# Dilated attention's probabilities: turned by VectorE in 32x32 squares and placed through DRAM, in place of TensorE transposes

## The reference, cut to what matters

```python
# per pattern: tokens of one residue modulo dil, in blocks of BLK = 128
s = einsum('bnqhd,bnkhd->bnhqk', q, k_prev_and_own) * 64 ** -0.5     # 128 queries x up to 256 keys
s = where(valid, s, -inf)
m = max(s); e = exp(s - m); l = sum(e)
o = einsum('bnhqk,bnkhd->bnqhd', e / l, v_prev_and_own)
lse = m + log(l)         # the three patterns' outputs are then weighted by softmax(lse)
```

## Time and profile before

| what | before |
|---|---|
| median of 3 runs | 3045.55 us (3045.34 to 3045.76) |
| profiled execution, its span | 3043.6 us |
| TensorE, VectorE, ScalarE, GpSimd busy | 99%, 69%, 35%, 64% |
| DMA | 301.71 MB in 367379 packets, mean 99 GB/s |
| TensorE's mean granted clock | 0.999 of full |

### The profile page before, as it was taken

How to read it: one execution, slowest core, us unless ns; L and a number is a source line. 1 busy time by engine, 2 the same in 40 slices (tenths; PEclk the granted TensorE clock), 3 DMA queues, 4 the chain that set the end, 5 groups by cost and what they waited for, 6 DMA issues and landing times.

```text
span 3043.6 us, 40003 instructions
## 1 busy us (share of the span) xinstructions
PE 3025.0 (99%) x14420; PEld 2448.4 (80%) x14420; DVE 2085.4 (69%) x2848; ACT 1057.5 (35%) x1911; POOL 1951.7 (64%) x1630
## 2 busy tenths in 40 slices
PE   8999999999999999999999999999999999999999
PEld 7777888888888888778888888888888777788887
DVE  6656585556888865565665558888769988797223
ACT  4223253333444421233343334444331345302112
POOL 5632458888999557433558878998545544486574
PEclk9999999999999999999999999999999999999999
DMA  5112234446444221112144456544111100111112
GB/s 167 51 42 50 74 108 160 152 153 246 154 152 166 82 84 51 48 43 87 50 140 153 152 187 213 154 148 151 47 44 49 35 28 22 32 49 49 46 63 83
DMA packets 367379, 301.71 MB, mean 99 GB/s; under 512 B 66640, under 2 KB 302160, under 8 KB 365648
## 3 DMA queue, kind: packets, MB, share of 16 engines
q1 hardware_dynamic: 318432, 222.33, 24.0%
q10 hardware_dynamic: 48752, 76.83, 7.3%
HBM read 223.29 MB, written 72.68 MB: 97 GB/s over the span
## 4 chain that ended last, share of the span: by engine, by line
PE 97%; DVE 2%; ACT 0%; issue 0%; DMA 0%; SPq 0%; DVEq 0%; ACTq 0%
PE ring L1581 14%; PE ring L1583 14%; PE ring L1582 14%; PE ring L1862 4%; PE ring L1863 4%; PE ring L1864 4%; PE ring L1895 4%; PE ring L1897 4%; PE ring L1896 4%; PE aux L1581 3%; PE aux L1583 3%; PE aux L1582 3%; PE aux L1895 2%; PE aux L1897 2%; PE aux L1896 2%; PE aux L1862 2%
## 5 line engine op out<-in xcount | busy, mean ns | idle before, releaser
L1288 POOL TENSOR_TENSOR w_hi<-w_raw,ones_r 128x512 fp32r<-128x512 f32 (+3 forms) x296 | 326.4, 1103 | 589.9 <-PE ring L1583 516.5
L1291 POOL TENSOR_TENSOR w_lo<-w_raw,w_hi 128x512 fp32r<-128x512 f32 (+3 forms) x296 | 382.5, 1292 | 23.2
L1581 PE MATMUL ring<-Q_hi,w_hi 128*128 128x512 f32 x752 | 300.1, 399 | 0.0
L1583 PE MATMUL ring<-Q_hi,w_lo 128*128 128x512 f32 x752 | 293.3, 390 | 0.0
L1582 PE MATMUL ring<-Q_lo,w_hi 128*128 128x512 f32 x752 | 293.0, 390 | 0.0
L1581 PE MATMUL ring<-P_hi,w_hi 128*128 128x512 f32 x656 | 268.2, 409 | 1.6 <-DVE P_lo L2716 1.2
L1583 PE MATMUL ring<-P_hi,w_lo 128*128 128x512 f32 x656 | 256.3, 391 | 0.0
L1582 PE MATMUL ring<-P_lo,w_hi 128*128 128x512 f32 x656 | 256.0, 390 | 0.0
L3211 DVE SCALAR_TENSOR_TENSOR conv_out<-conv_in,taps,conv_out 128x1021 f32<-128x1021 f32 (+29 forms) x120 | 188.0, 1614 | 0.2
L1581 PEld LDWEIGHTS ring<-Q_hi,w_hi 128*128 128x128 f32 x752 | 141.1, 188 | 54.0 <-issue 26.3
L1583 PEld LDWEIGHTS ring<-Q_hi,w_lo 128*128 128x128 f32 x752 | 141.2, 188 | 30.2
(11 more groups left out here) (494 smaller groups left out, 8536.5 us busy)
## 6 DMA issues: line engine op xcount, KB each, us to landing
hid_scratch<-stages SPq DMA_DIRECT2D x196, 256.0 KB, 2.1
w_raw<-in_w_in SPq DMA_DIRECT2D x84, 512.0 KB, 3.9
w_raw<-in_w_down SPq DMA_DIRECT2D x64, 512.0 KB, 3.8
p_slot<-hid_scratch ACTq DMA_DIRECT2D x50, 512.0 KB, 4.7
q_slot<-hid_scratch ACTq DMA_DIRECT2D x48, 512.0 KB, 4.7
w_raw<-in_w_up SPq DMA_DIRECT2D x36, 512.0 KB, 4.8
up_raw<-in_w_up SPq DMA_DIRECT2D x28, 512.0 KB, 5.2
p_slot<-first_scratch ACTq DMA_DIRECT2D x12, 1024.0 KB, 7.3
```

The costliest lines, as they stand in the source:

```text
L1288: g.tensor_tensor(w_hi[:, slot, ks], w_raw[:, slot, ks], one.broadcast_to([P, width, P]), ALU.mult).then_inc(w_hi_ready, 1)
L1291: g.tensor_tensor(w_lo[:, slot, ks], w_raw[:, slot, ks], w_hi[:, slot, ks].bitcast(F32), ALU.subtract).then_inc(w_ready, 1)
L1581: t.matmul(o, wh, xh, start=first, stop=False)
L1583: return t.matmul(o, wl, xh, start=False, stop=last)
```

## The change

The transposes on TensorE are gone. The probabilities stay in the PSUM banks `turned`: VectorE writes the masked scores there, ScalarE runs exp in place there. A new job `send`, five chunks after each stop's place, has VectorE turn each bank of 128x512 into `probs` in SBUF: its transpose turns each 32x32 square in place, so the squares themselves are not yet where a 128x128 transpose would have them. ScalarE then stores the 512 KB of `probs` to a DRAM scratch of two buffers, and at the next stop, when the store has landed and the previous probabilities have been used, it loads them in four transfers of 32 partitions each, in runs of 32 numbers, into `probs_t`. `attend` waits for all four. ScalarE works a stop for both units at once (outputs first, then the loads, then the exps). Some semaphores are merged (`eps_made` and `ones_set`, `swap_cleared`, `left_made`), and waits that spoke of `probs_taken` now speak of `probs_turned`.

```diff
-STEPS, LAG = 8, 2
+STEPS, LAG, SEND_LAG = 8, 2, 5
+SQUARES = 4
@@ weave
             put(m0 + k // KC, k % KC, "step", unit, i)
+            put(m0 + (k + SEND_LAG) // KC, (k + SEND_LAG) % KC, "send", unit, i)
@@ weave, unit 5
         put_a(8 + 8 * i, "step", 5, i)
+        if i < stops_of(5):
+            put_a(8 + 8 * i + SEND_LAG, "send", 5, i)
@@
+    probs_d = nc.dram_tensor("probs_scratch", (2, P, S), F32, kind="Internal").ap()
@@ TensorE
-        def turn_probs(l, unit, j):
...
-                    mm = t.transpose(turned[buf][:, 256 * e + at + b * P:256 * e + at + b * P + P], probs[:, buf, e, at + b * P:at + b * P + P], ident[:])
-            mm.then_inc(probs_turned, 1)
@@ attend
-            pe.wait_ge(probs_taken, no + 1)
+            pe.wait_ge(probs_back, 16 * SQUARES * (stops_before(l, unit, j * stops_of(unit) // STEPS) + 1))
@@ ScalarE, exp_block
-            act.wait_ge(max_ready, step_no(l, unit, j) + 1)
+            act.wait_ge(max_ready, step_no(l, unit, j | 1 if stops_of(unit) == 2 else j) + 1)
             for e in range(2):
-                x_ = probs[:, buf, e, at:at + n]
+                x_ = turned[buf][:, 256 * e + at:256 * e + at + n]
@@
+        def send_probs(l, unit, i):
+            no = stops_before(l, unit, i)
+            act.wait_ge(probs_turned, step_no(l, unit, blocks_of(unit, i)[-1]) + 1)
+            act.dma_start(probs_d[no % 2], probs[:].rearrange("q x e k -> q (x e k)")).then_inc(probs_sent, 16)
+
+        def fetch_probs(l, unit, i):
+
+            no = stops_before(l, unit, i)
+            act.wait_ge(probs_sent, 16 * (no + 1))
+            act.wait_ge(attended, step_no(l, unit, blocks_of(unit, i)[0]))
+            squares = probs_d[no % 2].rearrange("(a t) (x b j) -> b t x a j", a=SQUARES, b=SQUARES, j=32)
+            for b in range(SQUARES):
+                to = probs_t[32 * b:32 * b + 32].rearrange("t x e k -> t (x e k)").rearrange("t (x a j) -> t x a j", a=SQUARES, j=32)
+                act.dma_start(to, squares[b]).then_inc(probs_back, 16)
+
+        def attention_stop(l, parts):
+            for unit, i in parts:
+                if i >= 2:
+                    for j in blocks_of(unit, i - 2):
+                        take_attended(l, unit, j)
+            for unit, i in parts:
+                if 1 <= i <= stops_of(unit):
+                    fetch_probs(l, unit, i - 1)
+            for unit, i in parts:
+                if i < stops_of(unit):
+                    for j in blocks_of(unit, i):
+                        exp_block(l, unit, j)
@@ VectorE
-        def take_probs(l, unit, j):
...
-            v.tensor_copy(probs_t[:, j % 2, :, 0:n], turned[j % 2].rearrange("p (e k) -> p e k", e=2)[:, :, 0:n]).then_inc(probs_taken, 1)
+        def turn_probs(l, unit, i):
+
+            blocks = blocks_of(unit, i)
+            dve.wait_ge(exped, 2 * step_no(l, unit, blocks[-1]) + 2)
+            dve.wait_ge(probs_sent, 16 * stops_before(l, unit, i))
+            for x in range(2):
+                mm = v.transpose(probs[:, x].rearrange("q e k -> q (e k)"), turned[x])
+            mm.then_inc(probs_turned, len(blocks))
@@ take_scores
+            dve.wait_ge(probs_turned, step_no(l, unit, blocks_of(unit, s * stops_of(unit) // STEPS)[0]))
             dve.wait_ge(scored, step_no(l, unit, last_of_stop(unit, s)) + 1)
             for e in range(2):
-                v.tensor_tensor_reduce(out=probs[:, buf, e, half:half + n], in0=scores[e][:, col:col + n], in1=m, scale=1.0, scalar=-3.0e38,
+                v.tensor_tensor_reduce(out=turned[buf][:, 256 * e + half:256 * e + half + n], in0=scores[e][:, col:col + n], in1=m, scale=1.0, scalar=-3.0e38,
                                        op0=ALU.add, op1=ALU.max, accum_out=row_stat[:, unit, s, e:e + 1]).then_inc(masked, 1)
@@ VectorE, woven
                     for unit, i in unit_parts(*args):
-                        if 1 <= i <= stops_of(unit):
-                            for j in blocks_of(unit, i - 1):
-                                take_probs(l, unit, j)
                         if i < stops_of(unit):
                             for j in blocks_of(unit, i):
                                 take_scores(l, unit, j)
+                elif kind == "send":
+                    turn_probs(l, *args)
```

More of the change, by code:

```diff
@@ L243, with stops_before @@
 HN3_AFTER = {DOWNS - 4: (0,), DOWNS - 3: (1, 2), DOWNS - 2: (3, 4), DOWNS - 1: (5, 6)}
-STEPS, LAG = 8, 2
+STEPS, LAG, SEND_LAG = 8, 2, 5
+SQUARES = 4
 def stops_of(unit):
     return 2 if unit % GROUPS == 2 else 4
+def stops_before(l, unit, i):
+    return sum(stops_of(u) for u in range(UNITS)) * l + sum(stops_of(u) for u in range(unit)) + i
 def unit_parts(unit, i):
@@ L757, in two_blocks @@
     consts_made = sem("consts_made")
-    eps_made = sem("eps_made")
-    ones_set = sem("ones_set")
+    ones_made = sem("ones_made")
     w_hi_ready = sem("w_hi_ready")
@@ L808, in two_blocks @@
     exped = sem("exped")
-    probs_taken = sem("probs_taken")
+    probs_sent = sem("probs_sent")
+    probs_back = sem("probs_back")
     attn_taken = sem("attn_taken")
@@ L1267, in _ @@
         const_settled()
[L1268 to L1271, removed]
+        g.memset(ones[:], 1.0).then_inc(ones_made, 1)
+        pool.wait_ge(ones_made, 1)
+        g.tensor_tensor(ones_r[:], ones[:], ones[:], ALU.mult).then_inc(ones_made, 1)
+        pool.wait_ge(ones_made, 2)
         one = ones[:, 0:1].rearrange("p (a b) -> p a b", a=1)
@@ L1377, in prepare @@
             g.memset(rope_c[:], 1.0).then_inc(rope_set, 1)
-            g.memset(swapped_rows[:], 0.0).then_inc(swap_cleared, 1)
+            g.memset(swapped_rows[:], 0.0).then_inc(rope_set, 1)
         def attention_consts(l):
@@ L1692, in attention_stop @@
         def attention_stop(l, parts):
-            for unit, i in parts:
-                if 1 <= i <= stops_of(unit):
-                    for j in blocks_of(unit, i - 1):
-                        turn_probs(l, unit, j)
             for unit, i in parts:
@@ L1940, in _ @@
             turn_x(i)
-        pe.wait_ge(eps_made, 1)
+        pe.wait_ge(ones_made, 2)
         for l in range(DEPTH):
@@ L2314, in woven @@
                 elif kind == "step":
-                    for part in unit_parts(*args):
-                        attention_stop(l, *part)
+                    attention_stop(l, unit_parts(*args))
+                elif kind == "send":
+                    send_probs(l, *args)
                 elif kind == "pool":
```

31 lines of the change are left out of this document (8 added, 23 removed).

## The result

The changed kernel takes 3120.07 us (median of 4 runs, 3114.27 to 3121.46) against 3045.54 us for the kernel before (4 runs, 3045.34 to 3045.76): a ratio of 1.024, interval 1.0227 to 1.0252. It is slower, as forecast, but by 75 us and not by 17.6, and 14 us above the end of my range.

What follows compares the result with a forecast made beforehand. TensorE, a nearly full queue of matmuls, was taken as the bound. Waits of 53.6 us against 36 saved gave 17.6 slower: 3043.6 + 17.6 + 2.0 = 3063 us, range 3022 to 3106.

Steps and rivals of the forecast that it cites:

- wait at v before unit 5: TensorE's transposes of v: VectorE waits for exps and turns before taking v, so TensorE waits 3.9 us.
- the clock: TensorE's granted clock: a lower one after the new waits was named as a possible cost and put at nothing.
- Saved on TensorE: TensorE's 280 transposes of L1657 removed: 36 us taken as saved, between 37.0 by busy time and 35 by starts.
- Other waits for VectorE: TensorE's waits for VectorE beyond those at v and a 0.3 us PSUM bank wait: no cost given.
- The sizes of turn, exps, issues, store and pieces: Per stop: turn 1.4 us, four exps 1.9, four issues 2.8, store landing 3.0; pieces of 128 B 14 ns each.
- The round: ScalarE's in-order loop of fetch, exps, VectorE's turn and store landing: 9.3 us each time.
- pitch: Time between attention stops on TensorE: 9.40 us before, 8.65 without the transposes.
- slipping fetch: ScalarE's loads of probabilities fall behind their stop, because the loop is longer than the time between stops.
- the walk: Stop-by-stop sum of TensorE's waits through the units: 24.3 us per layer, 48.6 both, 53.6 with 5 for other transfers.
- the second: Rival: ScalarE's loop is shorter than the time between stops, 8.1 us; 19.4 us faster, 3026; chance 0.19.
- The third: Rival: VectorE's turn takes 1.4 us a block, each loop 1.4 longer; 39 us more, 3102; chance 0.09.
- The fourth: Rival: 128 B pieces go as slowly as 512 B ones, a fetch takes 9.7 us; 3134 us; chance 0.11.

Runs made afterwards that it cites:

- e4: Changed kernel without the probabilities' store and loads; VectorE turns into two SBUF buffers, attention uses unplaced squares: 3026.87 us, 0.9939 of the kernel before.
- e2: Changed kernel with the turn and store of a unit's fourth stop four chunks later, behind VectorE's taking of v: 3093.0 us, 1.0152 of the kernel before.
- e5: Changed kernel with a stop's four loads issued from SyncE's queue in place of ScalarE's: 3068.16 us, 1.0075 of the kernel before.
- e1: Changed kernel with SyncE's six reloads of h issued two at a time over three panels, not all at once: 3116.16 us, 1.0231 of the kernel before.
- e7: Kernel before, with VectorE's scaling of v repeated four times ahead of the real one in units 1, 2, 4, 5: 3096.43 us, 1.0166.
- e9: Changed kernel with each load reading 32 whole rows of 4 KB, squares left unplaced: 3072.41 us, 1.008 of the kernel before.

## Why the prediction was wrong, step by step

The forecast had +17.6 us on the span, the trace +75.0. The step that failed most is the price of the wait at v before unit 5: 3.9 us from a quiet DMA, with SyncE's loads put at nothing, where 16 us were measured in each layer. Next comes the clock, put at nothing, where it cost 17. The steps in order:

- **Saved on TensorE, 36 us: failed.** It was 27.9 of busy time (e4). I added up the starts of the transposes and forgot their neighbour. After, the first attend starts 0.32 us behind the start of the last 128x512 matmul (300.32 to 300.64), where the first transpose started 0.23 behind it (284.75 to 284.98): the whole stop, from that start to the next 128x512 matmul's, went from 2.69 us (284.75 to 287.44) to 2.03 (300.32 to 302.35), 0.66 for six transposes where I had 0.75. At 0.11 each the 280 are 31 us; the last 3 I can't place. It is 8.1 us of the miss.
- **Other waits for VectorE, costed at nothing: failed.** The four small rows have 11.3 us after; e4 has 7.0 in the same rows and 2.3 at v. I had called the cushion thin at L1644; it is thin at the shares too, and I had priced none of it.
- **The sizes of turn, exps, issues, store and pieces on a quiet DMA: right.** The turn takes 0.7 us a block as taken. Four exps take 1.6 us where I had 1.9 (in PSUM 0.34 and 0.45 us each, against 0.40 and 0.49 in the earlier trace rows). Four issues take 2.8, and the store lands in 3.5 for 3.0. The pieces: ScalarE's DMA queue in 295.5 to 299 us (packets, MB, share of 16 engines) shows 0.899 x 16 x 3.5 us over 3903, 12.9 ns each, where I took 14.

```profile
q10 hardware_dynamic: 3903, 0.49, 89.9%
```

- **The round, 9.3 us against a pitch of 8.65, and the slipping fetch: right.** The round took 9.64, and from one stop's attends to the next were 8.8 to 8.95. Without the two long ones the waits are as walked: 23.8 at the attends and 51.3 for `v_feat`, less 31.8, less 0.5 of before, 42.8 in all; the walk had 53.6 less 7.8 at these two places, 45.8. By place it holds in the main: unit 5's attends waited 12.5 (13.6 walked), and of the six other waits at v four took 3.4 to 4.7 us, but unit 3's two only 1.7 and 1.2, where I had 3 to 4.
- **The wait at v before unit 5, 3.9 us: failed, the largest step.** It took 15.7 and 16.1 us, 24.0 more than walked. I gave other transfers 5 us spread over all rounds, from a mean DMA share of 0.22, and put SyncE's loads at nothing because the change doesn't touch their queue. But the transfers are not spread: the h reloads stand in one place, in the kernel before too, and there SyncE's queue had 73.8% of the 16 DMA engines' time (310 to 330 us) and the fetch's loads landed after 5.6 to 11.4 us. To look up what SyncE issues beside each fetch, and not the mean, was the missing step. The order that makes the wait is shown by e2 (27 us back, and the wait then at ScalarE's copy of v) and by e5 (no wait at v over 0.9 us). That the reloads make the fetch late is shown in part: spread out (e1), they left 9.4 and 8.1 us of it, and the time only 4 us less.
- **The clock, put at nothing: failed.** It cost 16.9 us of busy time: half of the 34.1 us that TensorE worked at 1.2 GHz, in the stretches at its eight waits of 3.4 us or more. The prediction named the cost as possible and took it for nothing since none shows in the trace before; but that trace has only one such wait, 7.1 us before the first matmul, which says little of a wait in the middle of work. e7 shows that waits alone do it, at 2.4 us for each of 4.

Together 8.1 + 11.3 + 24.0 + 16.9 and -3.0 for the walk are 57.3, of 57.4 missed. All but the last go the same way, so the direction owes nothing to errors that cancel.

The rivals: the second (a loop shorter than the pitch) is out by the round of 9.64. Its condition holds in e9, where the fetch keeps step, and there the time is 3072 and not 3026: TensorE's busy time is 11.3 us above e4's, and 25.9 us of waits are left. The third is out by 0.7 us a block. The fourth is out by 12.9 ns a piece; the rule of the Trainium skill, page "DMA: Bandwidth & Descriptors", section "Rules for kernel authors", against a transpose by plain DMA describes no cost of this size here, and no run has the hardware's own transpose to compare with; the turning inside 32 was VectorE's. Pieces against whole rows are still worth 48 us (e9), by their issues and their transfers together.

It stays open why an issue of a fetch stretches to 6.9 us when other transfers are in flight: e5 shows that it does so from either queue, and no run shows what it waits for. And no run took the reloads of h away from the fetches altogether; from e1 it is at least 6 to 8 us of the 16.

## What to carry to other kernels

In a kernel whose first engine is full, work taken off it comes back only as far as the next engine keeps up. TensorE's waits cost more than they last: on the mean a wait of 4 or of 16 us cost 2.4 to 2.6 us more here, so that 33 us in eight waits were dearer than 33 us in two. A round trip through DRAM is priced at its worst place, not at the mean: list what every queue has in flight beside each store and fetch. And where a fetch is late, ask which in-order programs stand behind it; here two did, and freeing one moved the wait to the other.

## What I had not expected of the hardware

- Eight waits of 2.0 us, put in on VectorE's side alone, raised TensorE's busy time by 9.5 us for the same instructions; eight of 4.2 us by 19.3; two of 16.5 us by 5.1. Not every wait of 2.0 us was followed by the lower clock: five were, three were not.
- An issue of a four-dimensional load takes 0.71 us at the median, 0.56 at the least and up to 6.86 us beside other transfers; with whole rows it is 0.44 at the median.
- An exp on 128x256 in place in PSUM takes 0.45 us, where it took 0.49 in SBUF.
- Reads of 128 B at a stride of 4 KB pass at 12.9 ns apiece.
